# Seven half-size products for most feature pairs of the first MLP's up projection

## The reference, cut to what matters

```python
hn = rms_norm(h, g_mlp_pre[i])                       # 512 x 1024
ff = jnp.square(jax.nn.relu(hn @ w_up[i])) @ w_down[i]   # w_up 1024 x 4096, w_down 4096 x 1024
h = h + rms_norm(ff, g_mlp_post[i])
```

## Time and profile before

| | us |
|---|---|
| median of 3 runs | 1450.24 |
| lowest, highest | 1449.41, 1453.47 |
| profiled execution, first to last instruction (span) | 1448.3 |
| TensorE busy in it | 1433.9 |
| VectorE, ScalarE, GpSimd busy | 829.5, 567.7, 214.0 |
| the first MLP's whole tiles and `w_down` | about 240 to 556 |

### The profile page before, as it was taken

One profiled execution on the slowest core, in us unless ns is written; L12 is line 12 of the kernel. 1 busy time (PEld: TensorE's weight loads), 2 busy tenths in 40 slices (PEclk: granted clock), 3 DMA queues, 4 the chain that ended last, 5 costly groups with the idle time before them and its releaser, 6 DMA issues.

```text
span 1448.3 us, 18117 instructions
## 1 busy us (share of the span) xinstructions
PE 1433.9 (99%) x7154; PEld 1188.5 (82%) x7154; DVE 829.5 (57%) x1255; ACT 567.7 (39%) x853; POOL 214.0 (15%) x139
## 2 busy tenths in 40 slices
PE   9999999999999999999999999999999999999998
PEld 6776898888888888887799888888888888888887
DVE  5777488444434346786696736544463755535554
ACT  5345545323223124544464546323241533323320
POOL 4175322000000012430052104000020000000000
PEclk9999999999999999999999999999999999999999
DMA  6222123433323322222211211323332323332332
GB/s 238 88 74 73 59 73 102 115 94 98 102 88 102 102 88 73 88 71 67 82 59 33 71 44 59 116 88 102 98 92 88 102 92 102 98 102 91 99 98 78
DMA packets 36341, 129.86 MB, mean 90 GB/s; under 512 B 4040, under 2 KB 4296, under 8 KB 36256
## 3 DMA queue, kind: packets, MB, share of 16 engines
q1 hardware_dynamic: 35968, 128.44, 28.6%
q10 hardware_dynamic: 288, 0.26, 0.1%
HBM read 126.56 MB, written 2.10 MB: 89 GB/s over the span
## 4 chain that ended last, share of the span: by engine, by line
PE 94%; DVE 3%; ACT 1%; issue 1%; DMA 0%; POOL 0%; SPq 0%; DVEq 0%; POOLq 0%
PE P L1407 24%; PE P L1409 23%; PE P L1408 23%; PE P L1455 3%; PE P L1446 3%; PE P L1448 3%; PE P L1748 1%; PE P L1495 1%; PE P L1496 1%; PE P L1497 1%; PE P L1603 1%; PE P L1704 1%; DVE WL L2170 1%; PE P L1725 1%; PE P L1790 0%
## 5 line engine op out<-in xcount | busy, mean ns | idle before, releaser
L1827 ACT ACTIVATE WH<-WR 128x1024 fp32r<-128x1024 f32 x233 | 245.9, 1056 | 425.2 <-PE P L1409 361.3
L1407 PE MATMUL P<-AH,WH 128*128 128x512 f32 x856 | 342.4, 400 | 0.2 <-DVE BC L2514 0.2
L2170 DVE TENSOR_TENSOR WL<-WR,WH 128x1024 fp32r<-128x1024 f32 x217 | 291.0, 1341 | 78.8 <-ACT WH L1827 78.4
L1409 PE MATMUL P<-AH,WL 128*128 128x512 f32 x856 | 334.4, 391 | 0.0
L1408 PE MATMUL P<-AL,WH 128*128 128x512 f32 x856 | 334.1, 390 | 0.0
L1407 PEld LDWEIGHTS P<-AH,WH 128*128 128x128 f32 x856 | 161.1, 188 | 36.8 <-issue 4.5
L1409 PEld LDWEIGHTS P<-AH,WL 128*128 128x128 f32 x856 | 161.1, 188 | 34.3
L1408 PEld LDWEIGHTS P<-AL,WH 128*128 128x128 f32 x856 | 161.2, 188 | 32.0 <-issue 0.5
L1407 PE MATMUL P<-FH,WH 128*128 128x512 f32 x432 | 168.0, 389 | 0.0
L1408 PE MATMUL P<-FL,WH 128*128 128x512 f32 x432 | 168.0, 389 | 0.0
L1409 PE MATMUL P<-FH,WL 128*128 128x512 f32 x432 | 168.0, 389 | 0.0
(11 more groups left out here) (360 smaller groups left out, 2113.8 us busy)
## 6 DMA issues: line engine op xcount, KB each, us to landing
WR<-in_ws SPq DMA_DIRECT2D x233, 512.0 KB, 3.6
out<-Y SPq DMA_DIRECT2D x8, 256.0 KB, 2.0
H<-in_xT SPq DMA_DIRECT2D x3, 512.0 KB, 8.3
C<-in_const SPq DMA_DIRECT2D x1, 946.5 KB, 11.4
H<-in_xT SPq DMA_DIRECT2D x2, 256.0 KB, 4.2
PR<-in_pT SPq DMA_DIRECT2D x1, 512.0 KB, 4.4
WR<-in_ws SPq DMA_DIRECT2D x1, 384.0 KB, 4.4
GKU<-in_gku SPq DMA_DIRECT2D x1, 160.0 KB, 11.4
```

The costliest lines, as they stand in the source:

```text
L1407: e.matmul(P, wh, xh, start=start, stop=False)
L1409: ins = e.matmul(P, wl, xh, start=False, stop=stop)
L1827: e.activation(m.WH[:, c % NW, :], m.WR[:, c % NRAW, :], ACT.Copy).then_inc(*at.up("w_hi", "w_hi", c))
L2170: e.tensor_tensor(m.WL[:, c % NW, :], m.WR[:, c % NRAW, :], m.WH[:, c % NW, :].bitcast(F32), ALU.subtract).then_inc(*at.up("w_lo", "w_lo", c))
```

## The change

Tiles 0 to 7 stay as they were. The 24 others are made in 12 pairs (`pair`). A pair, 1024 x 256 weights by 512 tokens, is seen as a 2 x 2 matrix of blocks: the contracted features with even and odd tile number, the pair's two feature tiles, and the two halves of the tokens. Winograd's form of the seven-product scheme replaces the eight block products by seven, each 4 blocks of weights by 256 columns, three matmuls each (`mm_s`), in the order `SLOTS`. The four sums of inputs (`t_diff` on GpSimd, `t_u` on ScalarE, `t_2`, `t_3`, `t_4` on VectorE; split by `t_split`) are made once, beside tile 7 and the first 24 `w_down` blocks. The weight sums (`s_add` 1 to 4, 128 x 512 each, VectorE) are made for each pair from its two raw chunks; sums 1 to 3 are said with the `w_hi` of the unit ahead of the pair, sum 4 after the `w_lo` of the pair's plain unit. A pair has four units to convert (3.5 full ones) instead of two. The running sum in PSUM is copied between products (`s_snap`, ScalarE, 256 columns) and combined (`s_c11`, `s_c12`, `s_c22`, VectorE); ReLU and square become one VectorE instruction a tile (`up_first`, `up_second`, said after the block behind the pair), and the splits follow two and four blocks later (`up_split`). Two pairs stand in the first group of `w_down` blocks, after 24 and 48 of them; three in each of the next three groups, after 16, 32 and 48; one more follows the last of these. The groups have 6, 6, 6, 6 and 8 features and `F1` holds 12. A fourth raw buffer serves the chunks from the first pair to the last. `TB` is gone: ReLU writes `UB`, and the square works in place. `ple_load` waits for the last pair's last product, and `ple_in` is said four blocks later.

Cut to its core; moves of buffers and the split of `ffn` helpers in the second MLP (same instructions) are left out:

```diff
+FS = 12
+DOWN = ((0, 6), (6, 12), (12, 18), (18, 24), (24, 32))
+SLOTS = (1, 5, 6, 2, 7, 3, 4)
+PRODUCT_UNIT = {1: (0, 0), 2: (0, 1), 3: (3, 0), 4: (1, 1), 5: (2, 0), 6: (2, 1), 7: (1, 0)}
+            if c in starts:
+                self.pair_units[c] = {}
+                for kind in (2, 0, 3, 1):
+                    self.pair_units[c][kind] = len(self.units)
+                    self.units.append((kind, c))
+                c += 2
+            else:
+                self.unit_of[c] = len(self.units)
+                self.units.append((None, c))
+                c += 1
...
+        if sections:
+            extra.update((c, NRAW) for c in range(sections[0][0], sections[-1][0] + 2))
+        self.raw = []
+        self.raw_before = []
+        held = {}
+        for c in range(NCHUNK):
+            may = list(range(NRAW)) + ([extra[c]] if c in extra else [])
+            b = min(may, key=lambda q: held.get(q, -NRAW + q if q < NRAW else -NRAW - 1))
+            self.raw.append(b)
+            self.raw_before.append(held.get(b))
+            held[b] = c
+        self.raw_next = {b: c for c, b in enumerate(self.raw_before) if b is not None}
...
+    def convert(self, k):
+        self.converted = k
+        if k < len(self.units):
+            self.say("w_hi", k)
+            self.upper.append(k)
+            if k + 1 < len(self.units) and self.units[k + 1][0] == 2:
+                for j in (1, 2, 3):
+                    self.say("s_add", self.units[k + 1][1], j)
     def rest(self):
-        for c in self.upper:
-            self.say("w_lo_pool" if self.onpool else "w_lo", c)
-            if c + NRAW < NCHUNK:
-                self.say("w_load", c + NRAW)
+        for k in self.upper:
+            kind, c = self.units[k]
+            self.say("w_lo_pool" if self.onpool else "w_lo", k)
+            if kind == 0:
+                self.say("s_add", c, 4)
+            elif kind != 2:
+                self.load(c + 1 if kind == 1 else c)
         self.upper = []
+    def load(self, released):
+        c = self.raw_next.get(released)
+        if c is not None:
+            self.say("w_load", c)
+            if c + 1 < NCHUNK and self.raw_before[c + 1] is None:
+                self.say("w_load", c + 1)
...
+        for slot, k in enumerate(SLOTS):
+            self.tick()
+            if slot == 0:
+                p.x = self.ring()
+            if slot == 1:
+                p.z = self.ring()
+            if slot == 3:
+                p.y = self.ring()
+            for at, what, arg in ((1, "s_snap", 1), (2, "s_snap", 5), (3, "s_snap", 6), (4, "s_c11", None),
+                                  (5, "s_snap", 7), (6, "s_c12", None)):
+                if slot == at:
+                    self.say(what, p, arg)
+            if slot == 4:
+                self.close(p.y)
+            if slot == 6:
+                self.say("s_c22", p)
+                self.close(p.z)
+            if slot in (0, 3, 4, 6):
+                self.convert(self.converted + 1)
+                self.rest()
+            self.say("mm_s", p, k)
+            self.tick()
+        self.beside(post(p))
...
     def mlp1(self, post):
-        self.say("ple_load")
         A = [("A2", j) for j in range(8)]
         fu = lambda f: column("w_up", 128 * f)
@@ -741,23 +885,53 @@
             self.say("up1", f, t)
             self.close(t)
         out = self.head_halves("2", post, [fu(f) for f in range(6)], self.wide(fu(6), "A2"))
-        self.say("ple_in")
         self.paced(*(lambda f=f: up(f, out[f]) for f in range(7)))
-        up(7, self.tile(fu(7), A))
-        def down(g):
+        self.beside(self.forms("2"))
+        t = self.tile(fu(7), A)
+        up(7, t)
+        self.last_plain["2"] = t
+        def post(p):
+            f = p.f
+            self.say("up_first", p)
+            self.say("up_second", p)
+            self.close(p.x)
+            yield 2
+            self.say("up_split", f)
+            yield 2
+            self.say("up_split", f + 1)
+        def down(g, first, pairs_at):
+            taken = 0
+            f0, f1 = DOWN[g]
             for m in range(8):
-                t = self.tile([block("w_down", 128 * f, 128 * m) for f in range(8 * g, 8 * g + 8)],
-                              [("F1", f) for f in range(8 * g, 8 * g + 8)])
+                t = self.ring()
+                for f in range(f0, f1):
+                    if taken in pairs_at:
+                        if g == 0 and taken == 24:
+                            self.finish()
+                            self.banks = (0, 1, 2, 3, 6, 7)
+                            self.align()
+                        q = first + 2 * pairs_at.index(taken)
+                        self.pair("2", fu(q), fu(q + 1), q, post)
+                    self.block(t, block("w_down", 128 * f, 128 * m), ("F1", f), f == f0, f == f1 - 1)
+                    taken += 1
                 self.say("down1", m, t, g)
                 self.close(t)
-                if g == 3:
+                if g == len(DOWN) - 1:
                     self.say("square", "p2", m, 1)
-        for g in range(1, 4):
-            for f in range(8 * g, 8 * g + 8):
-                up(f, self.tile(fu(f), A))
-            down(g - 1)
-        down(3)
+            if taken in pairs_at:
+                q = first + 2 * pairs_at.index(taken)
+                self.pair("2", fu(q), fu(q + 1), q, post)
+        down(0, 8, (24, 48))
+        for g in (1, 2, 3):
+            down(g, 6 * g + 6, (16, 32, 48))
+        self.pair("2", fu(30), fu(31), 30, post)
+        self.say("ple_load")
+        self.finish()
+        self.banks = (0, 1, 2, 3)
+        self.paced(lambda: None, lambda: None, lambda: None, lambda: self.say("ple_in"))
+        down(4, None, ())
...
     def w_load(c):
-        if c == NRAW:
+        b, before = order.raw[c], order.raw_before[c]
+        if before == 0:
             w.wait_ge(*at("w_hi0", 1))
             w.wait_ge(*at("w_lo0", 1))
-        elif c > NRAW:
-            w.wait_ge(*at("w_hi", c - NRAW))
-            w.wait_ge(*at("w_lo", c - NRAW))
-        e.dma_start(m.WR[:, c % NRAW, :], d["ws"][c]).then_inc(*at.up(f"w_raw{c % NRAW}", "w_raw", c, by=16))
+        elif before is not None:
+            w.wait_ge(*at("w_hi", order.last_unit(before)))
+            w.wait_ge(*at("w_lo", order.last_unit(before)))
+        elif b >= NRAW:
+            w.wait_ge(*at("rbc", "2"))
+        e.dma_start(m.raw(b), d["ws"][c]).then_inc(*at.up(f"w_raw{b}", "w_raw", c, by=16))
...
+    def mm_s(p, k):
+        kind, half = PRODUCT_UNIT[k]
+        u = p.units[kind]
+        w.wait_ge(*at("w_hi", u))
+        w.wait_ge(*at("w_lo", u))
+        t = {5: p.z, 3: p.z, 2: p.y}.get(k, p.x)
+        P = m.bank[t.bank][:, cols(0)]
+        if k in (1, 5, 2):
+            free(t)
+        if k in (6, 7, 4, 3):
+            w.wait_ge(*at("snap", p.id, {6: 1, 7: 6, 4: 7, 3: 5}[k]))
+        if k in (5, 6, 7, 4):
+            j = {5: 1, 6: 2, 7: 3, 4: 4}[k]
+            w.wait_ge(*at("t_hi", p.s, j))
+            w.wait_ge(*at("t_lo", p.s, j))
+        for i in range(4):
+            xh, xl = m.form(p.s, k, i)
+            o = 512 * half + 128 * i
+            wh, wl = m.WH[:, u % NW, o:o + 128], m.WL[:, u % NW, o:o + 128]
+            e.matmul(P, wh, xh, start=k in (1, 5, 2) and i == 0, stop=False, skip_group_check=True)
+            e.matmul(P, wh, xl, start=False, stop=False, skip_group_check=True)
+            ins = e.matmul(P, wl, xh, start=False, stop=k in (2, 3, 4) and i == 3, skip_group_check=True)
+        ins.then_inc(*at.up("s_full", "s_full", p.id, k))
...
+    def s_add(c, j):
+        s = dict(order.found)[c]
+        x, y, z = m.raw(order.raw[c]), m.raw(order.raw[c + 1]), m.ws(s)
+        a11, a12, a21, a22, s1, s2 = x[:, 0:512], x[:, 512:1024], y[:, 0:512], y[:, 512:1024], z[:, 0, :], z[:, 1, :]
+        if j == 1:
+            w.wait_ge(*at("w_raw", c + 1))
+            w.wait_ge(*at("rbc", s))
+            if order.units_before(c) is not None:
+                w.wait_ge(*at("w_lo", order.units_before(c)))
+        elif j < 4:
+            w.wait_ge(*at("w_raw", c))
+            w.wait_ge(*at("s_add", c, 1))
+        else:
+            w.wait_ge(*at("s_add", c, 2))
+            w.wait_ge(*at("w_lo", order.pair_units[c][0]))
+        o, p, q, how = ((s1, a21, a22, ALU.add), (s2, a11, s1, ALU.subtract), (a21, a21, a11, ALU.subtract),
+                        (a12, a12, s2, ALU.add))[j - 1]
+        e.tensor_tensor(o, p, q, how).then_inc(*at.up("s_add", "s_add", c, j))
...
-    def up_hi(f):
+    def up_split(f):
         w.wait_ge(*at("up1", f))
-        if f >= 16:
-            w.wait_ge(*at("down1", f // 8 - 2, 7))
-        e.activation(m.FH1[:, f % 16, :], m.UB[:, f % 2, :], ACT.Copy).then_inc(*at.up("x_hi", "x_hi", "F1", f))
+        if f >= FS:
+            w.wait_ge(*at("down1", (f - FS) // 6, 7))
+        e.activation(m.FH1[:, f % FS, :], m.UB[:, f % 2, :], ACT.Copy).then_inc(*at.up("x_hi", "x_hi", "F1", f))
```

(30 more changed lines are left out.)

332 lines of the change are left out of this document (268 added, 64 removed).

## The result

The changed kernel takes **1469.73 us** (median of 4 runs, 1469.49 to 1470.59), the kernel before 1450.21 (4 runs, 1449.41 to 1453.47), side by side: ratio **1.0137** (95% interval 1.0123 to 1.0152), 1.4% slower. The forecast was 1462.4 in a range of 1449 to 1471. Its sign held and the time lies inside, 7 us above the forecast and just above the forecast's own range without its rivals, 1455 to 1469. Of the profiled executions, the span went from 1448.3 to 1468.1: +19.8.

What follows compares the result with a forecast made beforehand. TensorE, busy 99% of the span, was taken as the bound. Terms -9.6 + 8.9 + 0.9 + 9.9 + 0.1 + 2.0 = +12.2, with 1448.3 and 1.9, gave 1462.4 us; range 1449 to 1471, own range 1455 to 1469.

Steps and rivals of the forecast that it cites:

- Products: TensorE's matmuls in the 12 pairs: 84 of 256 columns replace 48 of 512, saving 0.80 us a pair, 9.6 us.
- Place 1: Start of the first w_down group: late load, queued sums and shared ReLU buffer delay the sixth block, +8.9 us (7.5 to 10.5).
- ring: First group's features: ReLU, square and low half follow one another through one buffer pair, 1.95 us a feature.
- Without the sums in the queue it would be about 4.7: Start of the first group: with no sums ahead of the squares, the delay falls from 8.9 to about 4.7 us.
- The first pair's snapshot: In the first pair, s_snap 1 waits for the last input split and the third product for that copy, +0.9 us.
- Place 2: Three group starts behind a pair: fifth and sixth blocks wait for that pair's features, +3.3 us each, 9.9 in all.
- The doubled pair: Near the end of the first MLP, two pairs close together delay one snapshot by +0.1 us.
- Clock: TensorE at 1.2 GHz after half-idle stretches: +2.0 us taken, bounded by 0 and 6 over four such times.
- waits and clock feed each other: Rival: all four places end in half clock (+4), place 1 +1.6, place 2 +3.6 more: 1471.6 us; chance 0.11.
- From the ends of the terms: Whole kernel: the forecast's own range without rivals, 1455 to 1469 us.
- All is hidden: Rival: sums and splits fit VectorE's idle time and only the products change, 1440.6 us; chance 0.13.
- One place only: Rival: place 1 costs 9.8 with the first pair's, place 2 boundaries 0 to 1 each, about 1452 us; chance 0.16.

Runs made afterwards that it cites:

- run 2: Changed kernel with the first pair's weight sums 1 to 3 said behind the squares, just before the conversion that reads them: 1465.26 us, ratio 1.0094 to the kernel before.
- run 4: Changed kernel with late first sums, pairs 8 blocks earlier and a second pair of ReLU buffers together: 1445.48 us, ratio 0.9956 to the kernel before.
- run 1: Changed kernel with the load into the extra buffer waiting for the input's last residual instead of rbc: 1464.9 us, ratio 1.0093 to the kernel before.
- run 3: Changed kernel with pairs after 24 and 40 blocks of the first group, 8, 24 and 40 of the next three: 1452.25 us, ratio 1.0018.
- run 6: Changed kernel with both splits of a pair said together, ahead of the w_lo and the sum: 1456.22 us, ratio 1.0038 to the kernel before.
- run 12: Changed kernel with late first sums and a second pair of ReLU buffers, pairs left where they were: 1461.5 us, ratio 1.0072 to the kernel before.
- run 5: Changed kernel with only the second pair of ReLU buffers back, sums and pairs unaltered: 1462.99 us, ratio 1.0087 to the kernel before.
- run 11: The changed kernel once more, unaltered: 1468.87 us, ratio 1.0113 to the kernel before.
- run 7: The kernel before with 18 extra unread matmuls ahead of down(3), shifting all later code: 1466.34 us, ratio 1.0106.

## Why the prediction was right, and where it was short

- **Products, -9.6.** Right: 12 x 0.80, 120.0 ns a matmul in every pair. The Trainium skill ("TensorE: Matmul & The Clock Gate", Wait — 56ns, not 53.3ns?) adds about 2.5 ns to a matmul's columns over 2.4 GHz; the estimate of 14 us from it does not hold for these matmuls, which take 11 ns more than that.
- **Place 1, +8.9.** Right by its steps, 8.8 measured: sixth block forecast at 257.4, measured 257.32; VectorE free for the sums at 243.9, measured 243.44; ring 1.95, measured 1.96; SP's next loads at 238.9, measured 238.92. "Without the sums in the queue it would be about 4.7", sixth block at 253.3: run 2 had it at 252.99. The stretch's +10.4 holds 1.5 us of half clock beside this.
- **The first pair's snapshot, +0.9.** It was 0. VectorE ended the last input split at 273.78 (forecast 273.6), but TensorE reached the pair at 271.79, not 270.4, by the 1.5 us of half clock: one miss hid the other. It was 1.1 in run 2, 1.0 in run 4, 0 in run 1. (The items listed for VectorE there add up to about 19 us, not 18.)
- **Place 2, +9.9.** Right: 3.3 forecast, 3.45 measured at each of three places, 10.3 in all. Runs 3, 6 and 12 put it where the forecast did.
- **The doubled pair, +0.1.** Measured 0.
- **Clock, +2.0.** This is the step that failed. I took one stretch's worth and called the waits at place 2 short. Measured: 1.5 at place 1 and 1.7 to 1.8 at each of the three places, 6.8 in the first MLP, above even my bound of 6. Each of the three had two waits with one block between them, 0.93 busy of 3 us, which is idler than the row I had priced the clock from the earlier trace rows. Run 6 shows it by taking the second wait away. At place 1 no run isolates it: in run 5, with the blocks closer together, the clock held, but in run 12 it fell there with still fewer waits.
- **Behind the MLP.** Nothing was forecast and 3.3 were found in the profiled pair of executions. By run 11 they come and go with the same code (1.6 there), and in run 7 a shift of the code did not bring them. What stays open is whether the changed kernel meets them more often than the one before; no run isolates that.
- **Sum.** -9.6 + 8.9 + 0 + 10.3 + 0 + 6.8 = +16.4, and 3.3 behind, for the +19.8 of the spans. The rival "waits and clock feed each other", at 0.11 and 1471.6, had the clock's term nearly right (6.0) and both waits too high; the forecast had the waits right and the clock wrong. The forecast's waits with that rival's clock would have given 1466.
- **The range.** "From the ends of the terms" the lower end, 1455, is right, but the upper ends add up to 1471.6 (place 1 +1.6, place 2 +3.6, clock +4), not 1469; that sum stands in the rival alone. The measured 1469.7 is above 1469, so it was the part added for the rivals that held it inside.
- **The rivals below.** "All is hidden" needed VectorE's idle share to help; run 3 shows the same load doing no harm once the distance is there, and the order, not the load, decided. "One place only" was right about place 1 and fell at place 2, where VectorE was not ahead when the pair ended.

## What to carry to other kernels

Cutting a phase's products moves its new work onto in-order queues, so count, for every fresh result, the time from its producer to its first use and what is said ahead of it: here 9.6 us saved were lost 2.7 times over at four places, and moving the pairs by 8 blocks, without removing an instruction, gave back 15.7. Where several results of one producer are wanted one after another, make them together: in run 6 the second wait, 5.3 us at three places, gave back 10.2, since TensorE's half clock had come on top. Before a buffer is taken to make room, see which ring it shortens: the second ReLU buffer was worth 0.56 us a feature.
